# Four reorderings in a model step on one core: an attention bias table spread head by head, recurrent weight loads, early state-space left operands, and the order of the latent heads

## The reference

```python
h = swiglu_half_step(h, ...)                     # ffn0
h = h + mamba2_mixer(rmsnorm(h, ssm_norm), ...)  # ssm
h = swiglu_half_step(h, ...)                     # ffn1
k_shared, v_shared = shared_kv(h, kv_norm, w_kv, k_norm)
h = swiglu_half_step(h, ...)                     # ffn2
h = h + sliding_window_attention(rmsnorm(h, attn_norm), k_shared, v_shared, ..., rel_bias, w_o)
h = swiglu_half_step(h, ...)                     # ffn3
```

```python
p = rms_norm(x, g_mix) @ w_in
y_a = mla_group(p[..., :672], positions, ...)    # 8 heads; q, k normed and turned by position
y_b = rwkv7_group(p[..., 672:], ...)             # 8 heads of 64, state of 64x64
x = x + concatenate([y_a, y_b]) @ w_o
x = x + peer_ffn(rms_norm(x, g_ffn), w_pq, sub_keys, expert_u, expert_v)
```

## Time and profile before

| | us |
|---|---|
| median of 3 runs | 2259.36 |
| lowest, highest | 2258.87, 2261.01 |
| profiled execution, its own time | 2254.98 |
| profiled execution, span | 2253.2 |
| PE busy | 2172.7 (96%) |
| DVE busy | 1471.9 (65%) |
| ACT busy | 1020.5 (45%) |
| mean DMA rate | 167 GB/s |

### The profile page before, as it was taken

The page is one execution under the profiler, slowest core; times in us unless marked ns, Lnnn a source line. Parts: engine busy times, 40 slices in busy tenths (PEclk is TensorE's granted clock), DMA queues, the critical chain, the costliest instruction groups (busy, mean ns, idle before and its releaser), DMA issues.

```text
span 2253.2 us, 42372 instructions
## 1 busy us (share of the span) xinstructions
PE 2172.7 (96%) x15414; PEld 1947.1 (86%) x15428; DVE 1471.9 (65%) x2790; ACT 1020.5 (45%) x1734; POOL 40.4 (2%) x40
## 2 busy tenths in 40 slices
PE   8999999999999999999998879999999999999999
PEld 7998997899889977899897547889888999999998
DVE  5557996655645556655675555989887666666665
ACT  4335775433433446433551343337634444444443
POOL 0000000000000000000000000110000000000000
PEclk9999999999999999999999989999999999999999
DMA  6555653455475534455431014443576666655554
GB/s 215 186 188 176 215 170 124 159 193 178 158 279 185 194 114 143 160 193 177 162 92 32 19 52 140 146 141 141 179 240 225 215 213 205 206 187 187 185 188 137
DMA packets 107550, 377.28 MB, mean 167 GB/s; under 512 B 11760, under 2 KB 17664, under 8 KB 107072
## 3 DMA queue, kind: packets, MB, share of 16 engines
q1 hardware_dynamic: 102848, 354.88, 47.7%
q0 software_dynamic: 4608, 21.15, 3.0%
HBM read 362.29 MB, written 13.69 MB: 167 GB/s over the span
## 4 chain that ended last, share of the span: by engine, by line
PE 88%; DVE 6%; ACT 2%; DMA 2%; DVEq 1%; issue 1%; ACTq 0%; POOL 0%; SPq 0%
PE bank L350 68%; PE bank L379 8%; PE bank L2495 3%; PE bank L1609 3%; DVE u_lo L565 1%; DVE w_lo L302 1%; DMA ring<-in_w 1%; ACT w_hi L297 1%; PE bank L598 1%; PE bank L616 0%; PE bank L2126 0%; DMA ring<-in_ssm_in 0%; DVE arena L1980 0%; DMA ring<-in_rwkv_in 0%; PE bank L876 0%
## 5 line engine op out<-in xcount | busy, mean ns | idle before, releaser
L302 DVE TENSOR_TENSOR w_lo<-ring,w_hi 128x1024 fp32r<-128x1024 f32 x581 | 702.6, 1222 | 423.2 <-ACT w_hi L297 420.5
L297 ACT ACTIVATE w_hi<-ring 128x1024 fp32r<-128x1024 f32 x581 | 605.9, 1057 | 635.1 <-PE bank L350 555.1
L350 PE MATMUL bank<-u_hi,w_hi 128*128 128x256 f32 x2568 | 730.7, 285 | 9.1 <-DVE w_lo L302 9.1
L350 PE MATMUL bank<-u_lo,w_hi 128*128 128x256 f32 x2568 | 728.4, 284 | 0.0
L350 PE MATMUL bank<-u_hi,w_lo 128*128 128x256 f32 x2568 | 728.4, 284 | 0.0
L350 PEld LDWEIGHTS bank<-u_hi,w_hi 128*128 128x128 f32 x2568 | 493.9, 192 | 20.3 <-DVE w_lo L302 8.0
L350 PEld LDWEIGHTS bank<-u_lo,w_hi 128*128 128x128 f32 x2568 | 494.1, 192 | 7.4 <-issue 0.5
L350 PEld LDWEIGHTS bank<-u_hi,w_lo 128*128 128x128 f32 x2568 | 494.0, 192 | 0.0
L350 PE MATMUL bank<-w_hi,x_hi 128*128 128x512 f32 x992 | 392.1, 395 | 8.2 <-DVE x_lo L1087 4.0
L350 PE MATMUL bank<-w_lo,x_hi 128*128 128x512 f32 x992 | 390.1, 393 | 0.0
L350 PE MATMUL bank<-w_hi,x_lo 128*128 128x512 f32 x992 | 387.6, 391 | 0.0
(11 more groups left out here) (312 smaller groups left out, 1758.9 us busy)
## 6 DMA issues: line engine op xcount, KB each, us to landing
ring<-in_w SPq DMA_DIRECT2D x264, 512.0 KB, 3.6
ring<-in_expert_u SPq DMA_DIRECT2D x128, 512.0 KB, 3.5
ring<-in_expert_v SPq DMA_DIRECT2D x128, 512.0 KB, 4.2
ring<-in_ssm_in SPq DMA_DIRECT2D x40, 512.0 KB, 4.4
gate_dram<-con SPq DMA_DIRECT2D x16, 576.0 KB, 2.8
arena<-gate_dram POOLq DMA_DIRECT2D x9, 1024.0 KB, 8.7
ring<-in_ssm_out SPq DMA_DIRECT2D x16, 512.0 KB, 3.8
ring<-in_w_o SPq DMA_DIRECT2D x16, 512.0 KB, 3.7
```

What stands on the lines that cost most here:

```text
L297: act.activation(w_hi[slot][:, :], ring[slot][:, :], ACT.Copy).then_inc(hi_made[slot], 1)
L302: dve.tensor_tensor(w_lo[slot][:, :], ring[slot][:, :], w_hi[slot][:, :].bitcast(F32), ALU.subtract).then_inc(freed[slot], 1)
L350: mm = pe.matmul(out, left[a], right[b], start=start and n == 0, stop=stop and n == 2, skip_group_check=True)
```

## The change

Four edits, independent of one another.

- The bias table: `bias_all` is gone. POOL copies each head's line from `line_dram` to its 128 places in `bias_dram`, 16 DMAs of 192 KB from DRAM to DRAM, each waiting for the one before; attention waits for all 17.
- The rwkv loads: tiles 4, 5 and 6 are issued before the wait for the split input and before w_wa and w_g.
- The state-space end: the first two x_hi are made by ACT before the eviction of the last tile, the first two x_lo by DVE before times_dt.
- The latent heads: halves are interleaved. PE's order, ACT's order and DVE's order within a pair change; outputs go to bank 3 of the group and their square sum to bank 2; the wait for mo_ready moves from the queries to the values; the output square sum of pair i stands behind a turn product of pair i + 1.

```diff
@@ -642,7 +642,6 @@
         k_root = area(7248, 2, T)
         rel = area(7760, 16)
         bias_line = area(7776, 384)
-        bias_all = area(8192, 16, 384)
         line_dram = nc.dram_tensor("line_dram", (16, 384), F32, kind="Internal").ap()
         bias_dram = nc.dram_tensor("bias_dram", (16, P * 384), F32, kind="Internal").ap()
         K_OUT, V_OUT, K_SUMS = bank[4:6], bank[7], bank[1]
@@ -956,6 +955,9 @@
                 for m in range(6, 9):
                     evict(G, m)
                 conv_silu(G, 4, 5)
+                if G == GROUPS - 1:
+                    left_hi(0)
+                    left_hi(1)
                 evict(G, 9)
 
             def decay_exps(G):
@@ -1007,7 +1009,7 @@
                 roots(G)
                 gates_of_group(G + 1)
             decay_exps(GROUPS - 1)
-            for b in range(6):
+            for b in range(2, 6):
                 left_hi(b)
             squares(GROUPS - 1)
             left_hi(6)
@@ -1138,10 +1140,10 @@
                 lo(s + 11)
             G, s = GROUPS - 1, SSM_TILES
             lo(s + 2)
+            left_lo(0)
+            left_lo(1)
             times_dt(G)
             causal_products(G)
-            left_lo(0)
-            left_lo(1)
             lo(s + 3)
             scores(G)
             for b in range(2, 5):
@@ -1174,11 +1176,10 @@
 
             pool.wait_ge(S("line_ready"), 1)
             pool.dma_start(line_dram, bias_line[0:16, :]).then_inc(S("line_moved"), 16)
-            pool.wait_ge(S("line_moved"), 16)
-            pool.dma_start(bias_all[:, :, :], line_dram.unsqueeze(0).broadcast_to([P, 16, 384])).then_inc(S("line_moved"), 16)
-            pool.wait_ge(S("line_moved"), 32)
-
-            pool.dma_start(bias_dram.rearrange("h (p y) -> p h y", p=P), bias_all[:, :, :]).then_inc(S("line_moved"), 16)
+            for head in range(16):
+                pool.wait_ge(S("line_moved"), 16 * (head + 1))
+                pool.dma_start(bias_dram[head:head + 1, :].rearrange("h (p y) -> h p y", p=P),
+                               line_dram[head:head + 1, :].unsqueeze(1).broadcast_to([1, P, 384])).then_inc(S("line_moved"), 16)
 
         def kv_tensor(pe):
             pe.wait_ge(S("kv_made"), 4)
@@ -1240,7 +1241,7 @@
         Q, SC, PT, OUT = bank[0:2], bank[2:4], bank[4:6], bank[6]
 
         def attn_sync(sp):
-            sp.wait_ge(S("line_moved"), 48)
+            sp.wait_ge(S("line_moved"), 16 * 17)
             sp.wait_ge(S("h_updated"), 4 * upd["attn"] + 1)
             def query(b, i):
                 load(sp, b, io["w_q"][bass.ds(2 * i + b, 1), :, :], "attn", i)
@@ -1539,12 +1540,13 @@
         def rwkv_sync(sp):
             for k in range(4):
                 load(sp, k, io["rwkv_in"][IN_TILES[k], :, :], "rwkv")
-            u_split_ready(sp, "rwkv")
-            sp.dma_start(w_wa, io["w_wa"]).then_inc(S("lora_loaded"), 16)
-            sp.dma_start(w_g, io["w_g"]).then_inc(S("lora_loaded"), 16)
             for k in range(4, 14):
                 slot, stage, i, nth = in_place(k)
                 load(sp, slot, io["rwkv_in"][IN_TILES[k], :, :], stage, i, nth)
+                if k == 6:
+                    u_split_ready(sp, "rwkv")
+                    sp.dma_start(w_wa, io["w_wa"]).then_inc(S("lora_loaded"), 16)
+                    sp.dma_start(w_g, io["w_g"]).then_inc(S("lora_loaded"), 16)
 
         def rwkv_tensor(pe):
             pe.wait_ge(S("h_updated"), 4 * upd["rwkv"] + 1)
@@ -1760,7 +1762,8 @@
             for n in range(2):
                 mm = pe.matmul(bank[5 + n][:, :], C("blk64"), flat(y_rw)[:, n * 512:(n + 1) * 512], start=True, stop=True)
             mm.then_inc(S("y_rw_summed"), 1)
-            head_squares(pe, 0)
+            head_squares(pe, 0, 0)
+            head_squares(pe, 0, 1)
             pe.wait_ge(S("y_rw_ready"), 1)
             for n in range(2):
                 mm = pe.matmul(bank[(4, 7)[n]][:, :], C("blk64"), flat(rw_tmp)[:, n * 512:(n + 1) * 512], start=True, stop=True)
@@ -2119,8 +2122,6 @@
                 pe.wait_ge(S("mla_loaded"), 32)
                 if i == 1:
                     pe.wait_ge(S("y_rw_rooted"), 1)
-                if i >= 2:
-                    pe.wait_ge(S("mo_ready"), i - 1)
             for c in range(3):
                 at = (3 * a + c) * QK
                 pe.matmul(head_banks(i)[a][Q_, 0:T], ring[i % 2][:, at:at + QK], lat[:, c, :], start=(c == 0), stop=(c == 2))
@@ -2134,6 +2135,8 @@
             mm.then_inc(S("mqk_done") if a == 0 else freed[i % 2], 1)
 
         def head_values(pe, i):
+            if i >= 2:
+                pe.wait_ge(S("mo_ready"), i - 1)
             for tt in range(TT):
                 for c in range(2):
                     at = i * 2 * P + c * P
...
@@ -2193,7 +2193,7 @@
             def outputs(i):
                 for a in range(2):
                     pe.wait_ge(S("mp_out"), 2 * i + a + 1)
-                    out, vs = group(i)[0][a * HD:(a + 1) * HD, :], slice(a * HD, (a + 1) * HD)
+                    out, vs = group(i)[3][a * HD:(a + 1) * HD, :], slice(a * HD, (a + 1) * HD)
                     v = v_pairs[:, i % 2, :, :]
                     pe.matmul(out[:, 0:P], v[:, 0, vs], m_prob_t[:, a, 0:P], start=True, stop=True)
                     pe.matmul(out[:, P:T], v[:, 0, vs], m_prob_t[:, a, P:2 * P], start=True, stop=False)
@@ -2202,52 +2202,64 @@
 
             def output_squares(i):
                 pe.wait_ge(S("mo_squared"), i + 1)
...
+            turn_halves(0, 0)
             for i in range(4):
                 more = i < 3
+                if i and more:
+                    head_queries(pe, i + 1, 0)
+                turn_halves(i, 1)
+                if i:
+                    output_squares(i - 1)
+                scores(i, 0)
+                if not i:
+                    head_queries(pe, 1, 0)
                 if more:
-                    for a in range(2):
-                        head_queries(pe, i + 1, a)
-                        head_keys(pe, i + 1, a)
+                    head_keys(pe, i + 1, 0)
+                scores(i, 1)
+                if more:
                     head_values(pe, i + 1)
+                    head_squares(pe, i + 1, 0)
+                    head_queries(pe, i + 1, 1)
+                    head_keys(pe, i + 1, 1)
                 turn_probs(i)
                 if more:
-                    head_squares(pe, i + 1)
+                    head_squares(pe, i + 1, 1)
+                    turn_halves(i + 1, 0)
                 outputs(i)
-                if more:
-                    turn_halves(i + 1)
-                output_squares(i)
-                if more:
-                    scores(i + 1)
+            output_squares(3)
 
         def mla_scalar(act):
...
-                    for a in range(2):
-                        square_head(act, i + 1, a)
+                    square_head(act, i + 1, 0)
+                exps(i, 0)
+                if i < 3:
                     keep_values(act, i + 1)
+                exps(i, 1)
+                if i < 3:
+                    root_head(act, i + 1, 0)
+                    square_head(act, i + 1, 1)
                 for a in range(2):
                     act.wait_ge(S("mp_turned"), 2 * i + a + 1)
                     act.activation(m_prob_t[:, a, :], group(i)[3 - a][:, 0:384], ACT.Copy).then_inc(S("mp_out"), 1)
                 if i < 3:
-                    for a in range(2):
-                        root_head(act, i + 1, a)
+                    root_head(act, i + 1, 1)
                 act.wait_ge(S("mo_done"), i + 1)
-                act.activation(mo_sq, group(i)[0][:, 0:T], ACT.Square).then_inc(S("mo_squared"), 1)
+                act.activation(mo_sq, group(i)[3][:, 0:T], ACT.Square).then_inc(S("mo_squared"), 1)
                 act.wait_ge(S("mo_summed"), i + 1)
-                rstd(act, mo_root, group(i)[1][:, 0:T], HD, stat[:, 14:15]).then_inc(S("mo_rooted"), 1)
+                rstd(act, mo_root, group(i)[2][:, 0:T], HD, stat[:, 14:15]).then_inc(S("mo_rooted"), 1)
 
         def mla_vector(dve):
             dve.wait_ge(S("lat_steps"), 3)
...
@@ -2261,24 +2273,26 @@
...
+            def scale_head(i, a):
+                dve.wait_ge(S("mqk_rooted"), 2 * i + a + 1)
+                for n, gain in enumerate(("g_qnorm", "g_knorm")):
+                    cols = slice(n * T, (n + 1) * T)
+                    ins = dve.scalar_tensor_tensor(qk_norm[Q_, a, cols], group(i)[a][Q_, cols], V(gain)[Q_, :],
+                                                   qk_root[Q_, a, cols], ALU.mult, ALU.mult)
+                ins.then_inc(S("mqk_normed"), 1)
+                dve.drain()
+
+            def turn_head(i, a):
+                dve.tensor_tensor(two(qk_cos[Q_, a, :]), two(qk_norm[Q_, a, :]), twice(cos_t), ALU.mult)
+                dve.wait_ge(S("mqk_turned"), 2 * i + a + 1)
+                dve.tensor_tensor(two(qk_sin[Q_, a, :]), two(group(i)[3 - a][Q_, :]), twice(sin_t), ALU.mult)
+                dve.drain()
```

(10 more changed lines are left out.)

## The result

The kernel after the change takes 2231.34 us in the median of 4 runs (2227.83 to 2233.85), the kernel before, on the same chip, 2260.03 (2258.87 to 2261.01): a ratio of 0.9873, 95% interval 0.9858 to 0.9889. The gain is 28.7 us; forecast were 25.7, and 2233.7 us. The profiled execution is the fastest of the four, with a span of 2226.0 us where before had 2253.2: 27.2 us.

The account below looks back on a forecast made before the run. TensorE held 88% of the chain, so only its idle or low-clock time could pay. Terms 5.7 + 6.2 + 5.2 + 8.6 = 25.7 us, taken from 2259.4, gave 2233.7 us; range 2228 to 2244.

Parts of the forecast that it names:

- Bias table: FFN2: 16 small copies replace two 3 MB transfers, weight loads no longer starve; gain 5.7 us, bounds 0 to 6.4.
- The twin comparison: FFN2 takes 8.41 us more than FFN1: 2.0 kv transposes, 6.4 waits for w_lo and low clock.
- rival (d): 16 serial bias copies outlast FFN2, over 11.9 us each before SP waits, 13.8 before a loss; 2272.5 us, chance 0.03.
- rival (a): Small bias copies starve FFN2's weight ring too, so the table's gain is gone; 2239.4 us, chance 0.11.
- The sign of being wrong: FFN2: the prediction is wrong if ring loads there stay over 6 us.
- The cause as I told it: FFN2: beside two 3 MB table transfers ring loads take 10.6 us against 3.6; bytes halve and never form a block.
- Recurrent entry: rwkv tile 4: earlier loads remove 3.64 us idle and 2.6 us low clock; gain 6.2 us, bounds 3.6 to 6.5.
- State-space: First output close: early left operands save 4.0 us idle and 1.4 low clock; 5.2 taken, bounds 3.5 to 5.5.
- Latent heads: Interleaved halves: a pair takes 14.1 us, not 16.94; 7.0 plus 1.6 low clock, gain 8.6, bounds 4 to 9.1.
- Rival (c): Latent heads gain nothing, another in-order wait replaces the old; 2242 us, chance 0.17 together with Rival (b).
- Rival (b): Low clock in four places (7.3 us) is paid elsewhere, DVE may set the latent pair; gain about 16, 2243 us.
- the last sentence of what would make the prediction wrong: Wrong if POOL's copies reach 800 us, FFN2 loads stay over 6 us, or a low-clock stretch appears where none was.

Follow-up runs that it names:

- burst: The changed kernel with its 16 DRAM-to-DRAM bias copies issued without waiting for one another, same bytes: 2232.35 us, ratio 0.9897 to the kernel before.
- via_burst: The changed kernel with the bias table's old 6 MB through SBUF, 16 copies in, one wait, 16 out: 2232.18 us, ratio 0.9890 to the kernel before.
- mla_alone: The kernel before with only the latent heads' new order: a gain of 9.3 us on 2256.7.
- after_again: The changed kernel, unchanged, timed and profiled a second time: 2232.01 us, ratio 0.9897 to the kernel before.
- act_old: The changed kernel with ScalarE's (ACT's) order of before in the latent heads: 2250.84 us, ratio 0.9978 to the kernel before.

## Why the prediction was right, step by step

**Bias table: 5.7 forecast, 6.7 measured.** The twin comparison held: all of FFN2's excess over its twin went but the kv blocks, which are 1.7 us (0.87 each in the chain, where the timeline's 1.04 has a drawn end) and not 2.0, so that even the term's top of 6.4 was 0.3 short. Taking 0.7 off for the first loads of the stage was wrong; they had slack. A copy took 4.1 us, not the 5.5 that the 256 KB rows gave, and ring loads 4.2, inside the 4 to 5 asked for. The sign of being wrong, loads over 6 us, was too strict: burst's took 7.3 us at no cost. The last copy was issued at 683, so the chain of 16 ended more than 100 us ahead of its use, and rival (d) never came near its 11.9 us a copy (its second price, 13.8, should be (190 + 25.7)/16 = 13.5 by its own sum); rival (a) failed on the same rows. The cause as I told it, bytes and block, was right in direction only: via_burst keeps bytes and way, issues without waits, and has 5.5 of the 6.7 us, so most of the gain hangs on the cut into pieces of 192 KB. By the Trainium skill (DMA: Bandwidth & Descriptors, Queues, rings and completion order), packets alternate between the queues that have work; the trace agrees for the 192 KB copies of via_burst, 1024 packets beside 1003 and 863 at shares of 42 to 48%. For the 3 MB store it shows 704 packets beside 471, 61.4 against 29.7%, and no row says whether the ring had a packet waiting on each engine all that time, so it neither agrees nor disagrees. The long delay behind a write to HBM, of which the Trainium skill warns (same page, Anatomy of one DMA, SWDGE path), didn't show in the copies, 14.3 us for 3 MB and 4.1 for 192 KB; the 24 KB write of the lines ahead of them took 6.1 us to land in after, longer than a copy of eight times its bytes, and why is open. The estimate by the Trainium skill's fit in that section was 2.5 us a copy; measured were 4.1 among ring loads.

**Recurrent entry: 6.2 forecast, 6.3 measured** (6.4 alone). Against the other kernels with the old order, where PE waited less for tile 4 or lost less clock than in before, it is 4.4 to 5.9. Both halves of the term, the wait of 3.64 and the tile at the lower clock, went; a tile takes 2.88 us where 2.9 was read off. Nothing came late behind it.

**State-space: 5.2 forecast, 5.7 measured**, which is the table's 5.5 and the 0.2 us by which this run started later. The first product came at 348.68, forecast 349.2. The next late operand was the one named, left operand 2 at 354.28, with a wait of 0.2 us.

**Latent heads: 8.6 forecast, 10.0 measured** in after, 8.1 in mla_alone and in after_again. The pair came out as walked, 14.10 against 14.1. From the first scores to the last the gain is 9.5 us (1277.5 to 1333.9 before, 1261.1 to 1308.0 after), 7.9 of it order if 1.6 is given to the clock as forecast. I had found 6.4 by idle time and 7.5 by start-to-start gaps and took 7.0 between them: that was the mis-sized choice, the gaps between starts were the right measure. With PE dense, the forecast said, the low clock behind the first pair goes; in after it did, but in mla_alone and after_again a stretch of 3.4 us stood there, at the first probabilities, and cost 1.4 us: most of the spread of 8.1 to 10.0. At the end the forecast said that the lower clock of 1336 to 1343 stays; it did, for 10.2 us in after and 13.6 in after_again. Rival (c), another in-order wait in the old one's place, didn't happen, but act_old is this rival built on purpose, and costs 19 us: that the gain hangs on ACT's order was not in the prediction.

**What no term had:** the 3.1 us given back in the inversion and 1.0 gained in attention. Rival (b) named the mechanism, a low stretch paid elsewhere, and the last sentence of what would make the prediction wrong named the sign, which came. Its size was off: 3.1 us, not 9.7, and it came where PE's waits were the same as before. The four terms measure 6.7 + 6.3 + 5.7 + 10.0 = 28.7 us, 3.0 above the forecast's 25.7; the later start (0.2), the inversion (3.1), attention (1.0) and the mix (0.8) take 1.5 of them back, which gives the 27.2 us of the spans. So part of the closeness is luck: terms 3.0 us too small and 1.5 us that no term had cancelled in part. The 28.7 us of the medians are from the set in which before was slowest (2260.0; 2255.8 to 2256.8 in the others). after_again gained 23.8, and the forecast of 25.7 lies between.

## What to carry to other kernels

Where a program has twin stages, their difference in time is the price of what one has and the other not, and it bounds an edit from above better than its waits do. A large transfer beside a stream of tiles should be costed in bytes that the stream falls behind against the tiles it has in hand, and cut into pieces of the tiles' order of size before its bytes or its time are worked on. When an order is changed on one engine of a chain, the order of each engine that feeds it has to be walked too: here the new order without ScalarE's part was a loss of 11 us in its stage and with it a gain of 10, while VectorE's part was worth 0.8 us.

## What the runs showed of the hardware that I had not expected

The granted clock fell in one run of the same kernel and stayed up in another at the same instructions behind the same wait of 1.29 us, and cost 1.4 us. In the inversion 1.5 us went with a difference of 0.4 us in when the stage starts (1140.01 to 1140.38). So a single profile of two kernels can differ by some 3 us that belongs to neither, and an edit's effect has to be read at its own stretch. Matmuls on zeros in PE's last waits kept the clock full through 48 us, but the next fall came all the same behind the next standstill of PE, 2.0 us at the end of the mix's first products; after had 1.8 us there and no fall.

And 6 MB in two transfers left the weight ring 121 to 134 GB/s, where the same 6 MB in 32 pieces without waits left it 165 to 174, though the whole moved about as fast (338 to 352 against 324 to 331 GB/s).
